# Delta rule on one Trainium2 core: a level's matrices waited for one by one, decay differences moved ahead, two projections joined

## What is computed

```python
def _gdn_scan(q, k, v, g, beta, S0):
    ...
    A = jnp.where(strict, bc[..., None] * kk * jnp.exp(jnp.where(strict, diff, 0.0)), 0.0)
    ...
    sol = lax.linalg.triangular_solve(A + jnp.eye(L, dtype=F32), rhs, left_side=True, lower=True,
                                      unit_diagonal=True)
    ...
    def step(S, xs):
        vn = U_i - jnp.einsum('bhld,bhde->bhle', W_i, S)
        o = jnp.einsum('bhld,bhde->bhle', qg_i, S) + jnp.einsum('bhls,bhse->bhle', qk_i, vn)
        S = gl_i[..., None, None] * S + jnp.einsum('bhld,bhle->bhde', kd_i, vn)
        return S, o
```

## Time and profile before

| | us |
|---|---|
| median of 3 runs | 6320.56 (6319.0 to 6321.11) |
| the profiled execution, its time | 6324.11 |
| its span | 6322.4 |

### The profile page before, as it was taken

How to read it: one execution, slowest core, us unless ns; L and a number is a source line. 1 busy time by engine, 2 the same in 40 slices (tenths; PEclk the granted TensorE clock), 3 DMA queues, 4 the chain that set the end, 5 groups by cost and what they waited for, 6 DMA issues and landing times. The chain is left out here.

```text
span 6322.4 us, 68907 instructions
## 1 busy us (share of the span) xinstructions
PE 5155.5 (82%) x24692; PEld 3512.5 (56%) x24692; DVE 3383.0 (54%) x7425; ACT 1396.0 (22%) x3134; POOL 3274.5 (52%) x3108
## 2 busy tenths in 40 slices
PE   6978867985888888788869788689958888888887
PEld 5767867983444444343357678679834444444432
DVE  3365534127666666666433655341276666666663
ACT  2231223111222122122222312231112221122221
POOL 2123410226777777777721234102167777777775
PEclk8888988998999999999978889889989999999999
DMA  4310011229999999999933100112299999999998
GB/s 141 121 43 8 1 41 45 70 93 332 409 403 400 397 391 401 374 391 393 387 127 121 43 8 1 41 48 68 96 340 407 402 399 401 390 404 393 405 404 347
DMA packets 507342, 1530.52 MB, mean 242 GB/s; under 512 B 57442, under 2 KB 155698, under 8 KB 504692
## 3 DMA queue, kind: packets, MB, share of 16 engines
q0 software_dynamic: 369536, 1342.48, 54.4%
q1 hardware_dynamic: 134804, 181.44, 8.6%
q10 hardware_dynamic: 2656, 2.11, 0.1%
HBM read 1520.75 MB, written 5.09 MB: 241 GB/s over the span
## 5 line engine op out<-in xcount | busy, mean ns | idle before, releaser
L2070 PE MATMUL pb<-vb,x_diags 128*128 128x512 f32 x5120 | 2499.8, 612 | 654.6 <-DMA vb<-in_p_v,x_idx 635.2
L1867 DVE CUSTOM_DVE_ANT_0 ub<-ub,h 128x1024 f32<-128x1024 f32 x1280 | 1567.4, 1225 | 1097.3 <-DMA ub<-in_p_u,x_idx 1087.5
L2070 PEld LDWEIGHTS pb<-vb,x_diags 128*128 128x128 f32 x5120 | 874.7, 190 | 1555.2 <-issue 1314.5
L1806 POOL DMA_INDIRECT ub<-in_p_u,x_idx x1280 | 1310.7, 1024 | 485.5 <-issue 362.5
L1806 POOL DMA_INDIRECT vb<-in_p_v,x_idx x1280 | 1298.6, 1015 | 409.4 <-issue 287.0
L2036 PEld LDWEIGHTS pb<-h2T,Wq 128*128 128x128 f32 x2560 | 459.5, 192 | 504.4 <-issue 501.5
L1990 ACT ACTIVATE x_diags<-identity,x_coefs 128x128 f32<-128x128 f32 x1280 | 416.5, 392 | 555.3 <-PE pb L2070 498.9
L2036 PE MATMUL pb<-h2T,Wq 128*128 128x128 f32 x2560 | 471.1, 276 | 2.4 <-DMA Wq<-in_p_wq 1.7
L239 PE MATMUL pb<-e_Whi,hS_hi 128*128 128x256 f32 x1280 | 382.3, 299 | 28.2 <-DVE e_Wlo L1688 28.2
L240 PE MATMUL pb<-e_Wlo,hS_hi 128*128 128x256 f32 x1280 | 359.2, 281 | 0.0
L241 PE MATMUL pb<-e_Whi,hS_lo 128*128 128x256 f32 x1280 | 358.9, 280 | 0.0
(11 more groups left out here) (403 smaller groups left out, 7880.9 us busy)
## 6 DMA issues: line engine op xcount, KB each, us to landing
adaW<-in_ada_w SPq DMA_DIRECT2D x40, 1024.0 KB, 10.3
e_Wg<-in_w_in SPq DMA_DIRECT2D x24, 1024.0 KB, 6.1
ub<-in_p_u,x_idx POOLq DMA_INDIRECT x1280, 6.6
vb<-in_p_v,x_idx POOLq DMA_INDIRECT x1280, 6.5
m_W<-in_w_in SPq DMA_DIRECT2D x16, 1024.0 KB, 5.7
Wq<-in_p_wq SPq DMA_DIRECT2D x8, 2048.0 KB, 17.2
g_W<-in_w_in SPq DMA_DIRECT2D x10, 1024.0 KB, 5.4
yT<-in_ada_w SPq DMA_DIRECT2D x8, 1024.0 KB, 5.5
```

What stands on the lines that cost most here:

```text
L1806: G.indirect_dma_start(ring[:, n % RING, :], None, table, bass.IndirectOffsetOnAxis(ap=idx[:, i % LIVE, s:s + 1], axis=0)).then_inc(in_[n ...
L1867: V.tensor_tensor_reduce(out=ub[:, n % RING, :], in0=ub[:, n % RING, :], in1=h2[:, t, :], scale=1.0, scalar=0.0, op0=ALU.mult, op1=ALU.add ...
L2070: last = mm(pb[2 * (t % 2) + j][:, :], diag[:, n % DRING, :], vb[:, n % RING, 512 * j:512 * j + 512], start=(h == 0 and s == 0), stop=(h = ...
```

## The change

1. The subtraction from Tv gets a semaphore of its own (`g_Tvu`), and from the second level on X waits for that one. The Y products now wait for the Tt of the level before.
2. The distances of step p+1 are issued on PE after the new values of step p and ahead of its state products, for both directions, and DVE masks them ahead of its last work of step p. Step 0 keeps its order.
3. The gate projection and the attention projection become one `project` of 5 chunks and 25 jobs with 6 banks and 2 raw weight buffers. The work of `finish_mixer` runs beside it: squares and root at the start on ACT and DVE, the gate's gain on POOL behind the low part of chunk 2, transposes on PE ahead of jobs 16 to 20. All jobs are now emptied by ACT. Delta rule and attention share a stage, and O's memory serves as yT[2] afterwards.

```diff
@@ layer
-                for b, build in enumerate((stage_mlstm, stage_deltanet, stage_attention)):
-                    yT[b] = sb(mix, f"yT{b}", [P, 4, TOK])
-                    with stage():
-                        build(l)
...
+                g_O = sb(mix, "g_O", [P, NT, 512])
+                yT[2] = g_O[:, :, :].rearrange("p t e -> p (t e)").rearrange("p (h s) -> p h s", h=4)
+                with stage():
+                    stage_deltanet(l, g_O)
+                    stage_attention(l, g_O)
@@ project
+                            if "gpsimd_after" in beside:
+                                beside["gpsimd_after"](pool, n, evA)
...
+                        if "scalar_first" in beside:
+                            beside["scalar_first"](act)
@@ new function
+        def finish_beside(l, scope, O, gate, evacuated):
...
+            TR_AT, EV_AT = 16, 16
+            def sync(sp):
+                sp.dma_start(g[:, :], A["g_norm_g"][l, None, :].to_broadcast([P, DH])).then_inc(s_in, 16)
+            def scalar_first(act):
+                for t in range(NT):
+                    S.activation(sq[:, 4 * t:4 * t + 4, :], Oh[:, 4 * t:4 * t + 4, :], ACT.Square).then_inc(s_sq, 1)
+                act.wait_ge(s_ms, 1)
+                S.activation(ms[:, :], ms[:, :], ACT.Sqrt).then_inc(s_rt, 1)
+            def scalar(act, i):
+                if EV_AT <= i < EV_AT + NT:
+                    t = i - EV_AT
+                    act.wait_ge(s_tr, t + 1)
+                    S.activation(yT[1][:, :, t * P:(t + 1) * P], v4(pb[6 + t % 2][:, :]), ACT.Copy).then_inc(s_ev, 1)
+            def vector(dve, evA):
...
+                for t in range(NT):
+                    dve.wait_ge(s_sq, t + 1)
+                    last = V.tensor_reduce(ms[:, 4 * t:4 * t + 4], sq[:, 4 * t:4 * t + 4, :], AX.X, ALU.add)
+                link(last)
+                V.tensor_scalar(ms[:, :], ms[:, :], 1.0 / DH, EPS, ALU.mult, ALU.add).then_inc(s_ms, 1)
+                dve.wait_ge(s_rt, 1)
+                link(V.reciprocal(ms[:, :], ms[:, :]))
+                for t in range(NT):
+                    dve.wait_ge(s_gg, t + 1)
...
+            def gpsimd_after(pool, n, evA):
+                if n == 2:
+                    pool.wait_ge(s_in, 16)
+                    for t in range(NT):
+                        pool.wait_ge(evA, evacuated(t))
+                        G.tensor_tensor(v4(gate[:, t, :]), v4(gate[:, t, :]), g[:, None, :].to_broadcast([P, 4, DH]), ALU.mult).then_inc(s_gg, 1)
+            def tensor_at(pe, i):
+                if TR_AT <= i < TR_AT + NT:
+                    t = i - TR_AT
+                    pe.wait_ge(s_y, t + 1)
+                    if t >= 2:
+                        pe.wait_ge(s_ev, t - 1)
+                    for h in range(4):
+                        last = tr(pb[6 + t % 2][:, h * P:(h + 1) * P], O[:, t, h * P:(h + 1) * P], ident)
+                    last.then_inc(s_tr, 1)
@@ stage_attention
-                    project("aproj", [(A["w_in"], O_AQ + CW * n) for n in range(3)],
...
+                    beside = finish_beside(l, wst, g_O, gz, lambda t: NT + t + 1)
+                    project("zaproj", [(A["w_in"], O_GZ + CW * n) for n in range(2)] + [(A["w_in"], O_AQ + CW * n) for n in range(3)],
...
+                                l, *weight_buffers(wst, "a", 2))
@@ stage_deltanet, PE
+                            def distances(p, d):
...
+                                if u >= 2:
+                                    pe.wait_ge(g_inc, u - 1)
...
                                         if j == 1:
                                             pe.wait_ge(g_Tv0, 2 * p + d + 1)
                                         else:
-                                            pe.wait_ge(g_T, 14 * p + 2 * (j - 1) + d + 1)
+                                            pe.wait_ge(g_Tvu, 10 * p + 2 * (j - 2) + d + 1)
...
                                         pe.wait_ge(g_Xc, n + 1)
-                                        if j == 1:
-                                            pe.wait_ge(g_T, 14 * p + d + 1)
+                                        pe.wait_ge(g_T, 14 * p + 2 * (j - 1) + d + 1)
...
                                     last.then_inc(g_vn, 1)
+                                if p + 1 < NT:
+                                    for d in both:
+                                        distances(p + 1, d)
@@ stage_deltanet, DVE
-                                            V.tensor_tensor(Tv[d][:, :], Tv[d][:, :], B[2][:, :], ALU.subtract)
+                                            V.tensor_tensor(Tv[d][:, :], Tv[d][:, :], B[2][:, :], ALU.subtract).then_inc(g_Tvu, 1)
...
                                     V.tensor_copy(Tv[d][:, :], B[2][:, :]).then_inc(g_vnc, 1)
+                                if p + 1 < NT:
+                                    for d in both:
+                                        masked(p + 1, d)
@@ stage_deltanet, end
-                    finish_mixer(1, l, O, gz, A["g_norm_g"], DH)
```

More of the change, by code:

```diff
@@ L960, in _ @@
                             last.then_inc(s_tr, 1)
+        def finish_beside(l, scope, O, gate, evacuated):
+            s_in, s_gg, s_sq, s_ms, s_rt, s_y, s_tr, s_ev = [sem(f"fin_{n}") for n in (
+                "gain_in", "gate_gained", "squared", "mean_square", "root", "gated", "transposed", "evac")]
+            sq = sb(scope, "fin_sq1", [P, NT * 4, DH])
+            g = sb(scope, "fin_g1", [P, DH])
+            ms = sb(scope, "fin_ms1", [P, NT * 4])
+            Oh = O[:, :, :].rearrange("p t (h e) -> p (t h) e", h=4)
+            TR_AT, EV_AT = 16, 16
[12 more added lines that the diff above has]
+            def vector(dve, evA):
+                link = chain("dve", dve)
+                for t in range(NT):
[8 more added lines that the diff above has]
+                    for h in range(4):
+                        hs = slice(h * DH, (h + 1) * DH)
+                        last = V.scalar_tensor_tensor(out=O[:, t, hs], in0=O[:, t, hs], scalar=ms[:, 4 * t + h:4 * t + h + 1], in1=gate[:, t, hs],
+                                                      op0=ALU.mult, op1=ALU.mult)
+                    last.then_inc(s_y, 1)
+            def gpsimd_after(pool, n, evA):
[10 more added lines that the diff above has]
+                        pe.wait_ge(s_ev, t - 1)
+                    for h in range(4):
+                        last = tr(pb[6 + t % 2][:, h * P:(h + 1) * P], O[:, t, h * P:(h + 1) * P], ident)
+                    last.then_inc(s_tr, 1)
+            return dict(sync=sync, scalar_first=scalar_first, scalar=scalar, vector=vector, gpsimd_after=gpsimd_after, tensor_at=tensor_at)
@@ L974, in stage_attention @@
                 with ExitStack() as wst:
[L975 to L977 removed]
+                    gz = sb(wst, "g_z", [P, NT, 512])
+                    beside = finish_beside(l, wst, g_O, gz, lambda t: NT + t + 1)
+                    project("zaproj", [(A["w_in"], O_GZ + CW * n) for n in range(2)] + [(A["w_in"], O_AQ + CW * n) for n in range(3)],
+                            [(n, "rows", t, None, [(gz[:, t, CW * n:CW * n + CW], 0, CW)], ACT.Silu) for n in range(2) for t in range(NT)] +
+                            [(2 + n, "rows", t, None, [(a[:, t, CW * n:CW * n + CW], 0, CW)], 1.0) for n in range(3) for t in range(NT)], beside, 6)(
+                                l, *weight_buffers(wst, "a", 2))
                 rot = sb(st, "a_rot", [P, 2, 4, ADH])
@@ L1405, in _ @@
                             pe.wait_ge(g_zero, 1)
+                            def distances(p, d):
+                                u, c = 2 * p + d, tile(d, p)
+                                r = slice(64 * d + 32, 64 * d + 64)
+                                B = bk[d]
+                                if u >= 2:
+                                    pe.wait_ge(g_inc, u - 1)
+                                mm(B[0][:, :], betar[r, sl(c)], sel[r, :, :].rearrange("p h s -> p (h s)"), start=True, stop=False)
+                                for h in range(4):
+                                    last = mm(B[0][:, sl(h)], sel[r, h, :], alpha[r, sl(c)], start=False, stop=(h == 3))
+                                last.then_inc(g_D, 1)
                             for p in range(NT):
@@ L1408, in _ @@
                                     u, c = 2 * p + d, tile(d, p)
-                                    r = slice(64 * d + 32, 64 * d + 64)
                                     B = bk[d]
[L1411 to L1416, removed]
+                                    if p == 0:
+                                        distances(0, d)
                                     if u >= 2:
@@ L1575, in stage_deltanet @@
                 tokens.close()
-                with ExitStack() as fst:
-                    gz = sb(fst, "g_z", [P, NT, 512])
-                    with ExitStack() as wst:
-                        project("gz", [(A["w_in"], O_GZ + CW * n) for n in range(2)],
```

(3 more changed lines are left out.)

21 lines of the change are left out of this document (13 added, 8 removed).

## The result

| | before | after |
|---|---|---|
| median of 3 runs | 6320.56 us | 6244.64 us (6242.77 to 6256.11) |
| profiled execution, its time | 6324.11 | 6244.64 |
| its span | 6322.4 | 6243.0 |

The ratio is 0.9885 with a 95% interval of 0.9863 to 0.9908: 1.15% faster, 76 us. The forecast was 6248. The sum of the prediction was -72.9 on the profiled execution, which gave -79.5. The two expert stages, which nothing touches, account for -10.4 of that: from the first load of the expert keys to the first issue of the next stage (or the end) they took 1780.5 + 1764.4 before and 1764.4 + 1770.1 after. The rest gave -69.1, so the sum was 3.8 too high in gain.

What follows compares the result with a forecast made beforehand. The last chain lay in the second layer's experts (POOL, DMA); the changed stretches were taken as serial. -30.5 + 3.2 - 56.8 + 10.8 + 0.4 = -72.9 us from 6324.11 gave 6251.2, less 3.55 for the median: 6248, range 6236 to 6262.

Steps and rivals of the forecast that it cites:

- Levels: Delta loop: X of direction 1 waits for the earlier subtraction from Tv, saving 0.61 us in 50 places, 30.5 us.
- the rival that it does nothing: Delta levels: PE's next wait (ACT's copy or AM from POOL) ends at the same time; total 6278, chance 0.05.
- Distances ahead: Eight step ends: key product of direction 1 waits for DVE's state update, +0.4 us each, +3.2 in all.
- PE runs both distances first: 563.71 + 3.9: Step end on PE: both directions' distances take 3.9 us, so state products start at 567.6.
- a sign that the prediction named: Step end in the profile after: the first transposes come 0.4 us later, not sooner.
- Joined project: First load to attention block: 83.9 us against 112.2, saving 28.4 per layer, 56.8 for two.
- The rival of a wait inside: Joined projections: POOL's queue more than 7 us late makes PE wait; 10 us for two layers, 6258; chance 0.12.
- Stage end: End of the joined stage: 108 semaphores cleared at 0.077 us each, 9.05 instead of 3.67; +10.8 us for two layers.
- rival one: Stage end: clearing is not its cost; a fixed price means the 10.8 us doesn't come back, 6237; chance 0.10.
- Tables: ACT loads the root's function once more, about 0.2 us exposed at the attention block's root; +0.4 for two layers.
- a sign against it: Expert stages, which nothing in the change touches, moving by themselves would show the prediction wrong; no size given.
- The rival of a low clock over whole jobs: Joined projections: PE at 1.2 GHz makes each job 2.83 us longer, 141 us in all, 6389; chance 0.02.

Runs made afterwards that it cites:

- experiments 2 and 3: Kernel after with distances back in old place (6254.67 us) or split by direction (6252.48); then with unread products added: 6231.85 without distances ahead, 6248.00 split, 6232.32 as made.

## Why the prediction was right, by its own steps

- **Levels: -30.5 forecast, -29.9 measured.** 40 periods of 6.17 became 5.57 or 5.58, and in each of the ten steps the stretch from direction 1's last subtraction from Tv to the copy of its new values fell by the same (11.74 to 11.14). The 0.61 between the two subtractions was the right row to price it by, no second wait was late behind it, and the rival that it does nothing is out.
- **Distances ahead: +3.2 forecast, +3.8 at the step ends (11.49 to 11.56, 12.52, 12.55 or 12.84), right in size by luck.** The reason given, the key products waiting for DVE's state, is there with 0.39 us, but the step that failed is "PE runs both distances first: 563.71 + 3.9". With it failed a sign that the prediction named: the first transposes start 11.28 behind the copy of direction 1's new values, where it was 11.38, so 0.10 sooner and not 0.4 later. Side by side the two directions' products, which use different groups of 32 rows, take 3.36, and this nearly pays for the wait: a step end without a clock fall costs 0.07, or 0.6 for eight. The other 3.2 are the three clock falls, which no step of the prediction had. The Trainium skill (TensorEngine Tiling (Array Packing), Key Properties) says that different tiles of the array can work at the same time; 3.36 against 2 x 1.95 agrees.
- **Joined project: -56.8 forecast, -52.8 measured.** Layer 1 gave 28.17 against 28.4, by the very terms of the sum: POOL's last gate multiplication, which waits for the gate's last evacuation, starts 846.09 - 807.15 = 38.9 after the first issue (forecast for that evacuation 38.6), and the rest takes 45.1 (forecast 45.3). Layer 2 gave 24.63: it took 86.09, since its first weights were there 6.97 after the first issue instead of 5.29, which is most of the 2.0 us between the two layers. In the ten traces with the joined project they were there 5.2 to 5.4 after it in layer 1 and 5.9 to 7.0 in layer 2 (the whole then takes 83.3 to 84.2 and 84.0 to 86.3); in the four with two projects 3.8 to 4.2 in both. The forecast took the old load and 0.35 for the gain's. Why the first weights come later, and more so in layer 2, was not tested. The sum took layer 1 twice; layer 2 should have been read by itself, where the old interval was already 1.5 shorter. The rival of a wait inside is out: the cover was 7 us, as reckoned.
- **Stage end: +10.8 forecast, +10.0 measured**, by 5.25 and 4.77. The run with 70 unused semaphores shows that it is their clearing; rival one is out. The 0.077 of the prediction held a break of 0.36 that the longer of its two ends has and the shorter has not, and in layer 2 the pace is 0.065 and not 0.071.
- **Tables: +0.4 forecast, +0.4 measured.** The last square ends at 895.10, the load of 1.28 starts at 895.12, and the root 0.01 behind it at 896.41; the root begins 5.19 after the block's first issue, where it was 4.99: 0.2, in both layers. By the rule of the Trainium skill (ScalarE: Activation LUTs, What ACT_TABLE_LOAD costs) of 2.66 per switch, 1.5 of it would have been exposed, as an estimate; the trace doesn't agree, since nothing stands ahead of the load or between the load and the root.
- **The rest.** First levels gave 134.8 in sum against 134.6, nothing. Loops -25.9, projections -52.8, stage ends +10.0 and the attention block -0.3 make -69.0, and the trace outside the experts gives -69.1; other stages moved by up to 3 us each and cancel. The remaining -10.4 of the profiled execution came from the experts, whose moving by themselves the prediction named as a sign against it; it bears on the time and not on the terms. Without them it would have been 6255.0, within the range too, while on the later chip the same kernel had a median of 6258 beside 6309 for the kernel before, 51 us less.
- The rival of a low clock over whole jobs is out: the granted clock was 1.00 over the joined project from 820 on. The clock did cost something, in the loops and in single products.
- A slip in the prediction's sums: the bad bounds that it names add up to 6262, not 6266. Nothing rests on it.

## What to carry to other kernels

Where one semaphore stands for two results, the distance between the two writes in the timeline is what a semaphore for the first alone gives back, provided the next wait in line has that much room: here 0.6 us in each of 50 places, met to within 2%. Merging two stages moves cost into the merged stage's end, which is priced by the count of semaphores that one engine clears, and the trace has that price directly, in the rows of the clears by their source line; two ends of different counts gave 0.077 here for 0.071. Reordering the work of an engine that was not idle there gained nothing; ask what the new neighbours do to the clock and to each other, and judge an edit of 3 us by its own stretch, since the whole time of this kernel moves by several times as much.

## What the runs showed of the hardware

- PE's granted clock fell from 1.00 to 0.50 with PE busy all the time by the profile, behind 3.36 us of products over 32 rows of two row groups, in 2 to 4 of the 8 places, by kernel and execution. Behind 1.95 us of them, followed by full products, it fell in none of the 32 step ends of the four kernels in experiments 2 and 3 that have no two side by side, nor in the 40 of the five others without part 2.
- An idle time of about 3.5 us cost 0.6 to 2.1 us of slow products behind it; products that nobody reads gave it back, 13.3 us over ten steps, with PE's busy time up and the span down.
- Clearing a semaphore on POOL takes about 0.07 us, 546 times in this program; on four engines side by side the end of a stage with 108 took 4.0 us instead of 8.9. A clear took 0.07 on ACT too, 0.08 on DVE and 0.12 on PE, which ended last.
